# Two sets of work moved and two feeding schedules changed in a two-block transformer kernel on one core

## The chip, the cores and the metric

The kernel runs on one core of a Trainium2 chip. The core has five engines, each with its own in-order queue of instructions: TensorE (PE, matmuls and transposes), ScalarE (ACT), VectorE (DVE), GpSimd (POOL), and SyncE (SP), which here only issues DMAs. Engines wait for each other on semaphores. The metric is the device time of the core in microseconds (us), lower is better.

## The reference

Two blocks work on 256 tokens of width 1024. The first has two layers: block attention (8 heads of 128) and a pooling mixer, each followed by an MLP of width 4096. The second block is cut down here to what matters for the change:

```
u = rms_norm(h)
z, xbc, dt, q_a, c_kv, k_rope, gate_ssd, gate_mla = split(u @ w_in)
y_ssd  = ssd_branch(z, xbc, dt) @ w_ssd_out        # ends in a group-wise RMS norm of y * silu(z), 4 groups
y_mla  = latent_attention(q_a, c_kv, k_rope) @ w_mla_out   # 16 heads
merged = sigmoid(gate_ssd) * y_ssd + sigmoid(gate_mla) * y_mla
h = h + merged @ w_o
h = h + cross_attention(rms_norm(h), rms_norm(mem))        # mem: 256 x 1024
h = h + mixture_of_experts(rms_norm(h))                    # 32 experts, 2 per token
```

## The kernel before

Activations lie transposed in SBUF: channels on the 128 partitions, the 256 tokens along the free axis, so 1024 channels are 8 tiles of 128x256. Every weight matrix is streamed through a ring of four slots. To multiply float32 values exactly enough, each operand is split in two `fp32r` parts. ACT writes the high part (L1457, a copy with rounding) and DVE the low part, the remainder (L2039, source minus high part); PE then runs three matmuls for each pair of tiles (`three`, L849 to L851): high x high, high x low, low x high. A weight chunk of 1024x256 is split in two halves of 128x1024 elements. There are four buffers for such halves, so ACT can be at most four halves ahead of PE: `high_half` waits for `units_done`. In ACT's and DVE's code, `feed(n)` means: now process the next n halves. The calls of `feed` are placed by hand between the other work, and so they set the order on both engines; nothing is reordered later.

Three stages are touched.

**First attention** (`attention(MOBA, ...)`, 8 heads). DVE's loop does in step i: mask head i's scores (L2158), take the maxima (L2165), normalise head i-1 (L2177, L2179), then what `meanwhile(i)` says, which is `feed`, and at last the remainder of the output of head i-4 (L2189). ACT does in step i: the exponentials of head i (L1550), the copy of the transposed probabilities of head i-2 (L1468), `feed`, and the high part of the output of head i-3 (L1570). On PE, in step i: scores of head i, transposes for head i-2, from step 5 on one k-tile of the output projection `wo1` for head i-5, then values of head i-3.

**Latent attention's entry.** PE projects queries (`qb`, L1186) and then keys and values (`kvb`, four parts, L1209); ACT copies both out of PSUM. Value products 3 and 4 use the PSUM banks of 1 and 2, after ACT has emptied them (L1837). `ssd_roots` (L1813) computes the four square roots of the group-wise norm of the other branch. The roots and the exponentials use different function tables of ACT, so there is a table load before and one behind. DVE inverts the roots (L2476), scales z (L2482), ACT writes its high part (`z_high`, L1827), DVE its remainder (`z_low`, L2489), and PE needs that for its first `sout` product.

**mout, memT, wo2.** PE computes `mout` in four chunks, each 48 matmuls; DVE gates each and adds it to `merged` (L2599 from PSUM, L2602 an add of two tiles in SBUF); ACT writes high parts of `merged` (`norm_parts`, L1478), DVE the remainders (`low_parts`, L2052), and PE multiplies with `wo2`, k-tile by k-tile as they come. Beside it, 16 transposes (L1257) bring `mem` into the channel layout; ACT copies them out (L1468), squares them (L1521), and POOL folds the 8 tiles of squares into one with three adds (`fold`, L2882); PE sums that over partitions (L820).

Of the kernel before, what the change touches and what calls it, by code (L numbers as in the profile page):

```python
# [31 lines left out]
P = 128  # L32
# [205 lines left out]
def plan():  # L238
# [65 lines left out]
    c.fill_each("memT", 4, (2, 3, 4, 5))  # L304
    for j in range(4):
        c.load(("wo2", j), kind="cols")
    c.fill_each("wo2", 4, (4, 5), lambda j: c.done(("wo2", j)))
    c.fill(0, "norm", 8)
# [27 lines left out]
def build_two_blocks(nc, a, out):  # L336
# [3 lines left out]
    with ExitStack() as ctx:  # L340
# [172 lines left out]
        def bank(b):  # L513
            return psum[:, b, :]
# [273 lines left out]
        def _(pe):  # L788
# [460 lines left out]
            for j in range(4):  # L1249
                project_split(c.ordinal["mout", j], open_bank("mout", j), head_of=None if j else lambda k: H1 + 2 * k)  # L1250
                if j == 0:
                    pe.wait_ge(s["mem_in"], 16)
                    for i in range(4):
                        b = open_bank("memT", i)
                        for m in range(2):
                            for tb in range(TB):
                                mm = pe.transpose(bank2(b)[:, m, tb * P:(tb + 1) * P],  # L1257
                                                  mem_in[:, tb, (2 * i + m) * P:(2 * i + m + 1) * P], ident)
                        mm.then_inc(full[b], 1)
# [176 lines left out]
        def _(act):  # L1436
# [376 lines left out]
            def ssd_roots():  # L1813
                wait_made("norm", 12)
                act.activation(std[:], std[:], ACT.Sqrt, bias=eps_col[:, 2:3],
                               scale=1.0 / (4 * P)).then_inc(s["ssd_roots"], 1)
                b = wait_full("norm", 13)
                act.activation(cb_sb[:], bank(b)[:, 0:TOK], ACT.Sqrt, bias=eps_col[:, 2:3],
                               scale=1.0 / (4 * P)).then_inc(made[b], 1)
                act.activation(std_col[:, 0, 1:2], eps_col[:, 0:1], ACT.Exp)  # L1820
# [9 lines left out]
            for part in range(4):  # L1830
# [8 lines left out]
                if part == 1:  # L1839
                    ssd_roots()  # L1840
# [10 lines left out]
            feed(2)  # L1851
            for j in range(4):
                copy_out(mem[:, 2 * j:2 * j + 2, :], "memT", j)
            for j in range(4):
                if j % 2 == 0:
                    feed(1)
                squares(8, j)
            feed(2)
            norm_parts("merged")
# [155 lines left out]
        def _(dve):  # L2015
# [225 lines left out]
            for j in range(9):  # L2241
# [6 lines left out]
                if j and j % 2 == 0:  # L2248
                    rope1(j // 2 - 1)
            attention(MOBA, CAUSAL, float(P) ** -0.5, True, one_tile,  # L2250
                      lambda i: feed((2, 2, 2, 0, 1, 1)[i] if i < 6 else 0))
# [342 lines left out]
            for j in range(4):  # L2594
# [9 lines left out]
                if j == 2:  # L2604
                    low_parts("merged", 0, 6)
            low_parts("merged", 6)
# [358 lines left out]
```

## Time and profile before

| | |
|---|---|
| time of the runs | 1382.43 us median of 3 (1382.18 to 1383.81) |
| profiled execution | 1382.18 us, its span 1380.4 us |
| PE busy | 1308.7 us (95%) |
| DVE busy | 1027.6 us (74%) |
| ACT busy | 869.0 us (63%) |
| POOL busy | 77.9 us (6%) |
| mean granted TensorE clock | 0.985 |
| the 16 transposes of `mem` | 863.23 us to 864.90 us from the span's start |

Times within the execution count from the span's start. The span runs from the first to the last instruction; 1.8 us of the profiled execution lie outside it. A matmul's record is longer than its share of the time, since matmuls overlap: what counts is how far apart they start (0.12 us for 128x256 at full clock). A row of a timeline stands for consecutive alike instructions, and the idle time ahead of it is in brackets with the instruction that ended it.

### The profile page before, as it was taken

To read this page: it belongs to the slowest core of one execution; us is meant where nothing else is said; L and a number is where in the kernel's file an instruction comes from. 1 tells how busy PE (TensorE), PEld (TensorE's weight loads), DVE (VectorE), ACT (ScalarE), POOL (GpSimd) and SP (SyncE) were. 2 spreads that over 40 slices of the span, in tenths; PEclk is the share of its full clock that TensorE was granted. 3 is DMA by queue.
4 is the path that set the end of the run, shared out by engine and by line. 5 is a ranking of instruction groups with operands and counts; after the bars stand their busy time and mean duration, and the time that the engine had idled before them with its cause. 6 is when DMAs were issued, how large, how long until landed. Compare 5 with 4: busy or idle time off the path is not lost.

```text
span 1380.4 us, 23725 instructions
## 1 busy us (share of the span) xinstructions
PE 1308.7 (95%) x9379; PEld 1202.8 (87%) x9382; DVE 1027.6 (74%) x1518; ACT 869.0 (63%) x1272; POOL 77.9 (6%) x81
## 2 busy tenths in 40 slices
PE   6999999999999998999999899999978999999993
PEld 6989999998999996999999888999976777777772
DVE  6676655568555657898988887875559999999994
ACT  5565444446444444676555766554458999999993
POOL 0000100001000000000001200110000111001113
PEclk9999999999999999999999999999989999999997
DMA  8644555553655541654544634555346999999972
GB/s 263 189 154 127 191 188 188 189 185 94 206 189 183 182 145 62 208 160 153 155 125 141 230 106 158 165 164 172 143 170 245 352 361 353 355 366 365 360 267 100
DMA packets 149676, 279.78 MB, mean 203 GB/s; under 512 B 13673, under 2 KB 122062, under 8 KB 136142
## 3 DMA queue, kind: packets, MB, share of 16 engines
q1 hardware_dynamic: 141886, 270.09, 56.8%
q0 software_dynamic: 7696, 8.41, 2.0%
q8 instruction: 63, 1.03, 0.3%
q14 instruction: 31, 0.25, 0.0%
HBM read 274.26 MB, written 21.50 MB: 214 GB/s over the span
## 4 chain that ended last, share of the span: by engine, by line
PE 74%; DVE 15%; ACT 6%; issue 3%; DMA 1%; ACTq 0%; DVEq 0%; POOLq 0%; POOL 0%; SPq 0%
PE psum L849 18%; PE psum L851 17%; PE psum L850 17%; DVE weights_parts L2627 3%; PE psum L1396 3%; PE psum L1395 3%; PE psum L1394 3%; DVE weights_parts L2039 3%; PE psum L1419 2%; ACT weights_parts L1903 2%; DVE arena L2421 2%; PE psum L1421 2%; PE psum L1420 2%; ACT weights_parts L1457 1%; ACT squares L1969 1%
## 5 line engine op out<-in xcount | busy, mean ns | idle before, releaser
L2039 DVE TENSOR_TENSOR weights_parts<-ring,weights_parts 128x1024 fp32r<-128x1024 f32 (+3 forms) x312 | 363.5, 1184 | 177.0 <-ACT weights_parts L1457 176.5
L1457 ACT ACTIVATE weights_parts<-ring 128x1024 fp32r<-128x1024 f32 (+3 forms) x312 | 308.8, 1009 | 179.3 <-PE psum L851 179.0
L849 PE MATMUL psum<-xnorm_parts,weights_parts 128*128 128x256 f32 (+1 forms) x932 | 269.8, 289 | 13.2 <-DVE xnorm_parts L2061 5.7
L850 PE MATMUL psum<-xnorm_parts,weights_parts 128*128 128x256 f32 (+1 forms) x932 | 263.3, 283 | 0.0
L851 PE MATMUL psum<-xnorm_parts,weights_parts 128*128 128x256 f32 (+1 forms) x932 | 263.1, 282 | 0.0
L849 PEld LDWEIGHTS psum<-xnorm_parts,weights_parts 128*128 128x128 f32 (+1 forms) x932 | 175.8, 189 | 20.6 <-issue 12.3
L849 PE MATMUL psum<-hidden_parts,weights_parts 128*128 128x256 f32 x640 | 181.9, 284 | 2.7 <-DVE hidden_parts L2489 1.7
L849 PE MATMUL psum<-expert_cols,weights_parts 128*128 128x256 f32 x640 | 180.7, 282 | 1.7 <-DVE expert_cols L2052 1.2
L851 PE MATMUL psum<-hidden_parts,weights_parts 128*128 128x256 f32 x640 | 180.5, 282 | 0.0
L850 PE MATMUL psum<-hidden_parts,weights_parts 128*128 128x256 f32 x640 | 180.5, 282 | 0.0
L851 PE MATMUL psum<-expert_cols,weights_parts 128*128 128x256 f32 x640 | 178.6, 279 | 0.0
L850 PE MATMUL psum<-expert_cols,weights_parts 128*128 128x256 f32 x640 | 178.6, 279 | 0.0
L850 PEld LDWEIGHTS psum<-xnorm_parts,weights_parts 128*128 128x128 f32 (+1 forms) x932 | 176.0, 189 | 1.2 <-issue 1.0
L851 PEld LDWEIGHTS psum<-xnorm_parts,weights_parts 128*128 128x128 f32 (+1 forms) x932 | 176.1, 189 | 0.3
L849 PEld LDWEIGHTS psum<-hidden_parts,weights_parts 128*128 128x128 f32 x640 | 121.4, 190 | 3.5 <-issue 3.5
L849 PEld LDWEIGHTS psum<-expert_cols,weights_parts 128*128 128x128 f32 x640 | 120.1, 188 | 2.5 <-DVE expert_cols L2052 1.4
L850 PEld LDWEIGHTS psum<-hidden_parts,weights_parts 128*128 128x128 f32 x640 | 121.3, 190 | 0.0
L851 PEld LDWEIGHTS psum<-hidden_parts,weights_parts 128*128 128x128 f32 x640 | 121.3, 190 | 0.0
L851 PEld LDWEIGHTS psum<-expert_cols,weights_parts 128*128 128x128 f32 x640 | 120.2, 188 | 0.0
L850 PEld LDWEIGHTS psum<-expert_cols,weights_parts 128*128 128x128 f32 x640 | 120.0, 187 | 0.2
L2627 DVE TENSOR_TENSOR weights_parts<-expert_raw,weights_parts 128x1024 fp32r<-128x1024 f32 x94 | 110.6, 1216 | 4.5 <-ACT weights_parts L1903 4.4
L1903 ACT ACTIVATE weights_parts<-expert_raw 128x1024 fp32r<-128x1024 f32 x94 | 94.8, 1052 | 3.0 <-PE psum L1421 2.1
(410 smaller groups left out, 2514.5 us busy)
## 6 DMA issues: line engine op xcount, KB each, us to landing
expert_raw<-in_w_exp_down SPq DMA_DIRECT2D x35, 1024.0 KB, 7.6
ring<-in_mlp_w_up SPq DMA_DIRECT2D x32, 1024.0 KB, 5.5
ring<-in_mlp_w_down SPq DMA_DIRECT2D x32, 1024.0 KB, 4.8
ring<-in_w_in SPq DMA_DIRECT2D x30, 1024.0 KB, 5.4
ring<-in_w_exp_gate SPq DMA_DIRECT2D x23, 1024.0 KB, 5.3
ring<-in_w_exp_up SPq DMA_DIRECT2D x23, 1024.0 KB, 7.6
ring<-in_attn_w_qkv SPq DMA_DIRECT2D x12, 1024.0 KB, 6.3
expert_raw<-in_w_exp_gate SPq DMA_DIRECT2D x12, 1024.0 KB, 5.0
```

Source lines behind the costliest of these rows:

```text
L849: pe.matmul(out, lh, rh, start=start, stop=False, **more)
L850: pe.matmul(out, lh, rl, start=False, stop=False, **more)
L851: return pe.matmul(out, ll, rh, start=False, stop=stop, **more)
L1394: pe.matmul(bank2(n % 2), x_high, high[:, :, k, :], start=(kk == 0), stop=False)
L1395: pe.matmul(bank2(n % 2), x_low, high[:, :, k, :], start=False, stop=False)
L1396: mm = pe.matmul(bank2(n % 2), x_high, low[:, :, k, :], start=False, stop=(kk == KT - 1))
L1419: pe.matmul(y, a_high, high[:, cc], start=(k == 0), stop=False)
L1420: pe.matmul(y, a_low, high[:, cc], start=False, stop=False)
L1457: ins = act.activation(high, src, ACT.Copy)
L1903: act.activation(high, src, ACT.Copy).then_inc(s["unit_high"], 1)
L2039: ins = dve.tensor_tensor(low, src, high.bitcast(F32), ALU.subtract)
L2627: dve.tensor_tensor(low, src, high.bitcast(F32), ALU.subtract).then_inc(s["unit_low"], 1)
```

## The change

There are four edits; the arithmetic stays the same.

- The DVE schedule of weight halves in the first attention goes from (2, 2, 2, 0, 1, 1) to (2, 2, 2, 1, 1) for steps 0 to 5.
- `ssd_roots` is no longer called after the second key and value part; its five instructions stand right after the query part on ACT.
- The transposes of `mem` stand behind the third chunk of `mout` on PE instead of the first, and use banks 0 to 3 instead of 2 to 5. ACT feeds all six weight halves first, then copies `mem`, then writes the first six high parts of `merged`, then the squares, then the last two high parts.
- DVE writes all eight remainders of `merged` after the fourth sum instead of six of them after the third.

```diff
@@ plan()
     c.fill_each("mout", 4, (0, 1, 6, 7), lambda j: c.done(("mout", j)))
-    c.fill_each("memT", 4, (2, 3, 4, 5))
     for j in range(4):
         c.load(("wo2", j), kind="cols")
     c.fill_each("wo2", 4, (4, 5), lambda j: c.done(("wo2", j)))
+    c.fill_each("memT", 4, (0, 1, 2, 3))
@@ PE
                 project_split(c.ordinal["mout", j], open_bank("mout", j), head_of=None if j else lambda k: H1 + 2 * k)
-                if j == 0:
+                if j == 2:
                     pe.wait_ge(s["mem_in"], 16)
                     for i in range(4):
                         b = open_bank("memT", i)
@@ ACT
                 feed(2)
-            def ssd_roots():
-                wait_made("norm", 12)
-                act.activation(std[:], std[:], ACT.Sqrt, bias=eps_col[:, 2:3],
...
+            wait_made("norm", 12)
+            act.activation(std[:], std[:], ACT.Sqrt, bias=eps_col[:, 2:3],
...
                 feed(1 if part < 3 else 0)
-                if part == 1:
-                    ssd_roots()
                 if part == 2:
                     z_high(0)
...
             attention(LATENT, CAUSAL, one_tile, between2)
-            feed(2)
+            feed(6)
             for j in range(4):
                 copy_out(mem[:, 2 * j:2 * j + 2, :], "memT", j)
-            for j in range(4):
-                if j % 2 == 0:
-                    feed(1)
-                squares(8, j)
-            feed(2)
-            norm_parts("merged")
+            norm_parts("merged", 0, 6)
+            squares(8)
+            norm_parts("merged", 6, KT)
             feed(4)
@@ DVE
             attention(MOBA, CAUSAL, float(P) ** -0.5, True, one_tile,
-                      lambda i: feed((2, 2, 2, 0, 1, 1)[i] if i < 6 else 0))
+                      lambda i: feed((2, 2, 2, 1, 1)[i] if i < 5 else 0))
...
                                   ALU.add).then_inc(s["y_ready"], 1)
-                if j == 2:
-                    low_parts("merged", 0, 6)
-            low_parts("merged", 6)
+            low_parts("merged")
```

The order on DVE in the first attention, from the mask of head 3 on. L2158 is the mask, L2165 the maxima, L2177 and L2179 the normalisation, L2039 a weight remainder, L2189 the remainder of an output. Before:

```order
L2158 SCALAR_TENSOR_TENSOR arena<-psum,consts_sb 128x384
L2165 TENSOR_REDUCE smax<-arena 128x1 x2
L2177 RECIPROCAL srec<-ssum 128x2
L2179 TENSOR_SCALAR arena<-arena,srec 128x128
L2179 TENSOR_SCALAR arena<-arena,srec 128x256
L2158 SCALAR_TENSOR_TENSOR arena<-psum,consts_sb 128x384
L2165 TENSOR_REDUCE smax<-arena 128x1 x2
L2177 RECIPROCAL srec<-ssum 128x2
L2179 TENSOR_SCALAR arena<-arena,srec 128x128
L2179 TENSOR_SCALAR arena<-arena,srec 128x256
L2039 TENSOR_TENSOR weights_parts<-ring,weights_parts 128x1024
L2189 TENSOR_TENSOR xnorm_parts<-psum,xnorm_parts 128x256
```

The same place in the changed kernel, whose DVE lines are numbered six lower:

```order
L2152 SCALAR_TENSOR_TENSOR arena<-psum,consts_sb 128x384
L2159 TENSOR_REDUCE smax<-arena 128x1 x2
L2171 RECIPROCAL srec<-ssum 128x2
L2173 TENSOR_SCALAR arena<-arena,srec 128x128
L2173 TENSOR_SCALAR arena<-arena,srec 128x256
L2033 TENSOR_TENSOR weights_parts<-ring,weights_parts 128x1024
L2152 SCALAR_TENSOR_TENSOR arena<-psum,consts_sb 128x384
L2159 TENSOR_REDUCE smax<-arena 128x1 x2
L2171 RECIPROCAL srec<-ssum 128x2
L2173 TENSOR_SCALAR arena<-arena,srec 128x128
L2173 TENSOR_SCALAR arena<-arena,srec 128x256
L2033 TENSOR_TENSOR weights_parts<-ring,weights_parts 128x1024
```

A weight remainder now stands ahead of head 4's mask; behind the second one the remainder of head 0's output follows, as before.

The order on ACT between the query copies and the latent attention. L1457 is a weight half, L1833 and L1834 copy keys, L1468 copies values. Before:

```order
L1457 ACTIVATE weights_parts<-ring 128x512 x4
L1833 ACTIVATE arena<-psum 64x2x256
L1834 ACTIVATE arena<-psum 64x2x256
L1457 ACTIVATE weights_parts<-ring 128x1024
L1468 ACTIVATE arena<-psum 128x512 x2
L1457 ACTIVATE weights_parts<-ring 128x1024
L1815 ACT_TABLE_LOAD
L1815 ACTIVATE std<-std,eps_col 128x768
L1818 ACTIVATE cb_sb<-psum,eps_col 128x256
L1820 ACT_TABLE_LOAD
L1820 ACTIVATE std_col<-eps_col 128x1
L1833 ACTIVATE arena<-psum 64x2x256
```

And in the changed kernel (lines one lower from here on):

```order
L1457 ACTIVATE weights_parts<-ring 128x512 x4
L1814 ACT_TABLE_LOAD
L1814 ACTIVATE std<-std,eps_col 128x768
L1817 ACTIVATE cb_sb<-psum,eps_col 128x256
L1819 ACT_TABLE_LOAD
L1819 ACTIVATE std_col<-eps_col 128x1
L1832 ACTIVATE arena<-psum 64x2x256
L1833 ACTIVATE arena<-psum 64x2x256
L1457 ACTIVATE weights_parts<-ring 128x1024
L1468 ACTIVATE arena<-psum 128x512 x2
L1457 ACTIVATE weights_parts<-ring 128x1024
```

The five instructions of the roots moved ahead of one key copy, two value copies and two weight halves.

The order on ACT behind the latent attention, from the last weight half in it. L1468 copies the transposed `mem`, L1521 squares it, L1478 writes high parts of `merged`. Before:

```order
L1457 ACTIVATE weights_parts<-ring 128x1024 x2
L1468 ACTIVATE arena<-psum 128x512 x4
L1457 ACTIVATE weights_parts<-ring 128x1024
L1521 ACTIVATE squares<-arena 128x512 x2
L1457 ACTIVATE weights_parts<-ring 128x1024
L1521 ACTIVATE squares<-arena 128x512 x2
L1457 ACTIVATE weights_parts<-ring 128x1024 x2
L1478 ACTIVATE expert_cols<-arena 128x256 x8
```

And in the changed kernel:

```order
L1457 ACTIVATE weights_parts<-ring 128x1024 x6
L1468 ACTIVATE arena<-psum 128x512 x4
L1478 ACTIVATE expert_cols<-arena 128x256 x6
L1521 ACTIVATE squares<-arena 128x512 x4
L1478 ACTIVATE expert_cols<-arena 128x256 x2
```

The squares, which POOL's fold waits for, moved behind the sixth weight half and six high parts.

## Rows read from the trace of the kernel before

**Rows 1.** The page: busy us (share), instructions of TensorE.
```profile
PE 1308.7 (95%) x9379; PEld 1202.8 (87%) x9382; DVE 1027.6 (74%) x1518; ACT 869.0 (63%) x1272; POOL 77.9 (6%) x81
```

**Rows 2.** Timeline, PE: start us, us, engine, line, what [idle before <-releaser].
```profile
99.55 0.36 PE L849 MATMUL psum<-xnorm_parts,weights_parts 128*128 128x256 f32 x1 [0.71 <-DVE xnorm_parts L2189]
...
777.14 0.36 PE L849 MATMUL psum<-hidden_parts,weights_parts 128*128 128x256 f32 x1 [1.72 <-DVE hidden_parts L2489]
...
885.54 0.38 PE L849 MATMUL psum<-expert_cols,weights_parts 128*128 128x256 f32 x1 [1.24 <-DVE expert_cols L2052]
```

**Rows 3.** Timeline, DVE, first attention, heads 3 and 4.
```profile
96.04 0.55 DVE L2158 SCALAR_TENSOR_TENSOR arena<-psum,consts_sb 128x384 f32<-128x384 f32 x1
96.63 0.61 DVE L2165 TENSOR_REDUCE smax<-arena 128x1 f32<-128x128 f32 x2
...
97.84 1.23 DVE L2039 TENSOR_TENSOR weights_parts<-ring,weights_parts 128x1024 fp32r<-128x1024 f32 x1
98.98 0.42 DVE L2189 TENSOR_TENSOR xnorm_parts<-psum,xnorm_parts 128x256 fp32r<-128x256 f32 x1
```

**Rows 4.** Timeline, ACT, first attention, same stretch.
```profile
96.77 1.04 ACT L1457 ACTIVATE weights_parts<-ring 128x1024 fp32r<-128x1024 f32 x1
...
97.98 0.39 ACT L1550 ACTIVATE arena<-arena,smax 128x128 f32<-128x128 f32 x1
...
99.23 1.05 ACT L1457 ACTIVATE weights_parts<-ring 128x1024 fp32r<-128x1024 f32 x1
```

**Rows 5.** Timeline, PE, first attention, the next two rounds' first `wo1` matmul.
```profile
102.78 0.36 PE L849 MATMUL psum<-xnorm_parts,weights_parts 128*128 128x256 f32 x1 [0.64 <-DVE xnorm_parts L2189]
...
105.12 0.36 PE L849 MATMUL psum<-xnorm_parts,weights_parts 128*128 128x256 f32 x1
```

**Rows 6.** Windows: stretch, its us, busy us of each engine, PEclk, DMA.
```profile
774.00:777.00 3.00, 0.89 (x4) 0.52 (x4) 2.97 (x5) 2.82 (x5) 0.00 (x0) 1.00 1.02 408
777.00:782.00 5.00, 4.86 (x27) 4.88 (x28) 4.88 (x11) 1.41 (x6) 0.00 (x0) 0.66 0.97 380
```

**Rows 7.** Timeline, ACT, keys, values and roots before the latent attention.
```profile
764.86 0.59 ACT L1833 ACTIVATE arena<-psum 64x512 f32<-64x512 f32 x1 [0.29 <-PE psum L851]
...
767.03 1.09 ACT L1468 ACTIVATE arena<-psum 128x512 f32<-128x512 f32 x2
...
769.08 1.28 ACT L1815 ACT_TABLE_LOAD   x1
...
773.09 0.57 ACT L1833 ACTIVATE arena<-psum 64x512 f32<-64x512 f32 x1
...
775.12 0.62 ACT L1827 ACTIVATE hidden_parts<-arena 128x512 fp32r<-128x512 f32 x1
```

**Rows 8.** Timeline, PE, the third value product's first matmul.
```profile
767.79 0.38 PE L849 MATMUL psum<-weights_parts,xnorm_parts 128*128 128x256 f32 x1
```

**Rows 9.** Timeline, DVE, the first remainder of z.
```profile
776.20 0.68 DVE L2489 TENSOR_TENSOR hidden_parts<-arena,hidden_parts 128x512 fp32r<-128x512 f32 x1
```

**Rows 10.** Timeline, PE, the first matmul of `wo2`.
```profile
882.03 0.28 PE L849 MATMUL psum<-expert_cols,weights_parts 128*128 128x256 f32 x1
```

**Rows 11.** Timeline, DVE, sums and remainders of `merged`.
```profile
873.82 2.18 DVE L2602 TENSOR_TENSOR arena<-arena,rope_a 128x512 f32<-128x512 f32 x1
...
881.16 2.10 DVE L2052 SCALAR_TENSOR_TENSOR expert_cols<-arena,expert_cols 128x256 fp32r<-128x256 f32 x6
...
883.89 0.69 DVE L2602 TENSOR_TENSOR arena<-arena,rope_a 128x512 f32<-128x512 f32 x1
```

**Rows 12.** Timeline, ACT, copies and squares of `mem`, high parts of `merged`.
```profile
864.40 2.04 ACT L1468 ACTIVATE arena<-psum 128x512 f32<-128x512 f32 x4
...
871.83 1.13 ACT L1521 ACTIVATE squares<-arena 128x512 f32<-128x512 f32 x2
...
877.51 1.32 ACT L1478 ACTIVATE expert_cols<-arena 128x256 fp32r<-128x256 f32 x4
```

**Rows 13.** Timeline, POOL, the fold's first step.
```profile
873.05 2.39 POOL L2882 TENSOR_TENSOR squares<-squares 128x1024 f32<-128x1024 f32 x1 [20.45 <-ACT squares L1521]
```

More of the change, by code:

```diff
@@ L1812, in _ @@
                 feed(2)
-            def ssd_roots():
-                wait_made("norm", 12)
-                act.activation(std[:], std[:], ACT.Sqrt, bias=eps_col[:, 2:3],
[L1816 to L1820, printed above, removed]
+            wait_made("norm", 12)
+            act.activation(std[:], std[:], ACT.Sqrt, bias=eps_col[:, 2:3],
+                           scale=1.0 / (4 * P)).then_inc(s["ssd_roots"], 1)
+            b = wait_full("norm", 13)
+            act.activation(cb_sb[:], bank(b)[:, 0:TOK], ACT.Sqrt, bias=eps_col[:, 2:3],
+                           scale=1.0 / (4 * P)).then_inc(made[b], 1)
+            act.activation(std_col[:, 0, 1:2], eps_col[:, 0:1], ACT.Exp)
             def z_high(j):
```

## The prediction

> **What bounds the kernel now.** I read the page first. TensorE (PE) is busy 1308.7 of 1380.4 us [rows 1]; the work is one in-order stream of matmuls, and ScalarE (ACT) and VectorE (DVE) matter only where PE stands still for them. Then the timelines of ACT, DVE, PE and GpSimd (POOL) around the three places that the diff touches. There the reader is to see who is the last to arrive. In the first attention PE waits for DVE's remainders before the first output-projection matmuls [rows 2]. Before the second attention it waits 1.72 us for the first remainder of z [rows 2]. In the projection `wo2` it waits 1.24 us for two late parts of `merged` [rows 2]. Everything behind each place is PE work without slack (busy 95% over the whole span), so what PE loses there reaches the end; what ACT or DVE saves there doesn't, unless it was what PE waited for.
>
> **Edit 1, first attention, DVE: a weight remainder one head earlier.** In before, DVE takes head 4's mask, maxima, reciprocal and scaling from 96.04 to 97.84 and only then the weight remainder, for which ACT's high part (96.77 + 1.04 = 97.81) is just ready [rows 3, 4]. The high part doesn't come earlier after the change, since ACT's own order stays. So DVE stands from about 96.1 to 97.84 and does the remainder at the same time as before; the 1.8 us of head work come behind it, from 98.98. The maxima of head 4 end at 98.98 + 0.59 + 0.53 = 100.1 (before 97.2). ACT's exponentials of head 4 start then instead of at 97.98, and its next weight half follows 1.25 later (97.98 to 99.23): 101.4 to 102.45. DVE, now waiting for that one a head early too, does its remainder at 102.5 to 103.6 (the 1.14 of 97.84 to 98.98), then the remainder of head 0's output, 103.6 to 104.05, which stood at 98.98. PE's first `wo1` product follows 0.15 behind: 104.2 instead of 99.55, 4.65 us late. A part comes back: DVE's next round holds no weight remainder any more. In before PE took 3.23 us from 99.55 to 102.78, waits included, where an undisturbed round takes 2.34 (102.78 to 105.12) [rows 2, 5]. So 0.9 comes back and 3.8 us stay.
>
> **The clock behind it.** PE does almost nothing from 98.5 to 104.2 (one head's three transposes). What such a hole does to the granted clock is to be seen at 774 to 782: PE had 0.89 us of work in 3 us, and in the next 5 us the clock averaged 0.66 of full [rows 6], that is about 3.4 us at 1.2 instead of 2.4 GHz and some 1.7 us of work lost. For edit 1 I take 1.5 of that (bounds 0, if the low stretch falls into the hole itself, and 2.5, if it is longer). Edit 1: 3.8 + 1.5 = 5.3 us, bounds 3 and 6.3.
>
> **Edit 2, ACT: the four roots of the normalisation with their two table loads, 4.0 us (769.08 to 773.09), moved ahead of the keys and values.** In before they stood behind the value copies. Moved, they start when the query part of ACT's queue ends, at about 764.5, and run until 768.5. Then come the key copy that started at 764.86, a weight half, and the value copies of 767.03 [rows 7], all 4.01 - 0.29 = 3.7 us later (the 0.29 us of idle goes). PE's third value product uses the bank that these copies empty: 767.79 [rows 8] becomes 771.4, +3.6 us. What gives it back is that PE had time: ACT's second key copy (773.09) now waits for PE instead, which has done 24 matmuls at 0.12 us each by 774.4. From there copy, weight half and high part of z take 2.65 (the 2.03 from 773.09 to 775.12 and the part's 0.62): 777.15. The z remainder on DVE, at 776.20 before [rows 9], starts then, 1.0 us late, and PE and the attention's first maxima with it. The reciprocal for which DVE waited on the roots is done early and gains nothing, because the high part is last now. But the 3.6 us hole of PE brings the low clock onto the products behind it: up to 1.7 us later, of which about 1.1 reach the end. Edit 2: 1.0 + 1.1 = 2.1 us, bounds 0 and 3.5.
>
> **Edit 3, PE, ACT and DVE around `mout`, `memT` and `wo2`.** PE's 16 transposes move behind the third product. PE has the same work, so `wo2` could start at 882.03 as before [rows 10]; nothing on PE. The banks that they now use were emptied long before, nothing either. The order of the other two engines is what costs. First, the remainders of `merged` 0 to 5, done at 881.16 to 883.2 in before [rows 11], all come after the fourth sum. That sum can start 1.1 us earlier (about 882.1, when PE is done, instead of 883.17, one operation of 0.72 ahead of its add at 883.89), but the first remainder now ends at 883.5 + 0.35 or later, and PE needs it for its first matmul. A remainder is 0.35 us (2.10 for 6) and three matmuls are 0.36, so PE keeps that pace: it starts near 884.0 and its wait is 2.0 instead of 1.24, +0.8 us. This is the low bound.
>
> Second, the squares of `mem` slide from 869 to 873 towards the end. ACT's sixth weight half ends at about 875.7 (PE is through three products at 874.7), the four copies take 2.04, six high parts 0.33 each, four squares 0.57 each [rows 12]: 875.7 + 2.0 + 2.0 + 2.2 = 881.9. There POOL begins its fold. In before it began at 873.05 with a step of 2.39 us, and DVE's add of two tiles in SBUF at 873.82, which takes 0.69 alone, took 2.18 [rows 11, 13]: it ended 0.56 behind POOL's step, so it stood still until POOL let go. In the new order the fold meets that add again, 0.8 us into the same step: the fourth sum, now what PE waits for. It ends near 884.9 instead of 883.5, and the first remainder meets the second step and ends near 886.3. The Trainium skill ("SBUF — State Buffer", section "SBUF: two separate sides") says that a GpSimd operation and a VectorE operation with two SBUF inputs exclude each other for a whole instruction, and whoever starts first holds the port. The row agrees with a full stop, 1.49 us, rather than a shared rate. By that rule all hangs on POOL being 0.8 us ahead; were it behind the add, the add would be free and only the remainders would pay.
>
> Worked by rows: eight remainders are 2.8 us alone, and stops in DVE's stream over that fold were 1.5 for the add and, by its neighbours, about as much again for what followed. The last remainder ends at 883.5 + 2.8 + 3.0 = 889.3, PE's first half of `wo2` at 889.8. In before it was 885.54 + 0.7 = 886.25. That is +3.5 us. PE is idle from 882.03 to 886.4 in this, longer than in any of the holes above, so the low clock follows; a part lies beside DVE's slow stream, and I add 1.1. Edit 3: 4.6 us, bounds 0.8 and 5.5. The sum of squares on PE stands behind `wo2`'s first chunk, after the fold's end (887.7), so no further wait; ACT's next weight halves come about 1 us later, and two units are still ahead of PE.
>
> **Sum.** 5.3 + 2.1 + 4.6 = 12.0 us. The profiled execution took 1382.18 us for a span of 1380.4, the median of the runs is 1382.43, so 1382.2 to 1382.4 + 12.0 = 1394.3.
>
> **On the clock rule.** The Trainium skill ("TensorE: Matmul & The Clock Gate", Part 1) says that the low clock is the default and comes back after idleness. Read strictly, as a stretch with no work at all, edit 1's hole (which holds one set of transposes) would cost nothing and the sum would be 1392.8. The row at 774 to 777 shows a fall with 0.89 us of work in it, so I go by the row.
>
> **Rivals.**
> A, the clock stays high: the three holes cost only their own length, 3.8 + 1.0 + 3.5 = 8.3, 1390.6. For it: after the 1.24 us wait at 885.54 nothing fell. Against: the new holes are two to four times longer.
> B, only the queue delays count: POOL's fold starts late enough, or early enough, not to stand before the add, and edit 2 is hidden. 3.8 + 0.8 = 4.6, 1387.0. For it: edit 2 gives 2.6 of its 3.6 us back already by my count. Against: the 0.8 us by which the fold leads is worked out from six durations of one queue.
> C, the low clock lasts longer behind two of the holes, or the low bound of give-back in edit 1 holds: 6.3 + 3.5 + 5.5 = 15.3, 1397.6.
> D, not slower: the end of the fold's present collision pays. In before the fold stops DVE by 3.1 us at 873.8 to 879.8, and this is why the fourth sum starts at 883.17 rather than 882.1. If ACT delivers its weight half for DVE in the first attention ahead of the maxima (so that edit 1 fills idle time) and PE takes the parts of `merged` as they come, 1.1 us come out of the 1.24 us wait and 0.3 from ACT's idle slot: 1381.0. It decides only if edit 1 costs under 1.4 us; against it stands ACT's row at 96.77, behind which DVE must wait.
>
> **How the numbers follow.** Forecast 0.55, A 0.20, B 0.10, C 0.09, D or no difference 0.06. A measurement of this kernel can tell about 0.2% (2.8 us) from no change. B stays above that, so slower 0.93, within 0.2% 0.05, faster 0.02. The range, 1386.5 to 1397.5, takes in the forecast with its bounds, A and B, and leaves C and D outside, 0.15 in all.
>
> **What would show it.** In the first attention PE's first `wo1` matmul 4 to 5 us later than 99.55, and a low-clock stretch near 105. The two table loads at about 764.5, PE idle for over 3 us before the third value product, and the first `hidden_parts` product 1 to 2.5 us later by this edit alone. In `wo2`, one wait of 2 to 4.5 us at its first matmul in place of the 1.24 us wait at its 19th, with POOL's first step across DVE's fourth sum. I am wrong if these waits are there but DVE or PE had slack that takes them up, or if the fold doesn't meet the fourth sum.

## The result, and the profile after

| | before | after |
|---|---|---|
| median of the runs | 1383.12 us (1382.18 to 1384.13, 4 runs) | 1397.99 us (1396.04 to 1398.29, 4 runs) |
| profiled execution, its span | 1382.18, 1380.4 | 1396.05, 1394.2 |
| PE busy | 1308.7 | 1312.1 |
| mean granted TensorE clock | 0.985 | 0.980 |

The ratio is 1.0105 with the interval [1.0089, 1.0121]: 14.9 us slower. Forecast were 12.0 us and 1394.3 us, with a range up to 1397.5. The direction and the three places are right, the size is not: the time lies 0.5 us above the range. Of the 3.7 us between forecast and measurement, 2.9 are the size of the change; 0.8 is the starting point, since the forecast started from 1382.2 to 1382.4 and the median of before is 1383.12 here.

The timeline of PE in the changed kernel, at the starts of the three places and before the third value product. The first row is the wait ahead of head 3's transposes, the first of two in the first attention; the second, fourth and fifth rows answer to [rows 2], the third to [rows 8] (start us, us, line, what, [idle before <-releaser]):

```profile
101.88 0.52 PE L898 MATMUL psum<-consts_sb,arena 128*128 128x128 f32 x3 [2.48 <-DVE arena L2173]
...
105.15 0.55 PE L849 MATMUL psum<-xnorm_parts,weights_parts 128*128 128x256 f32 x1 [2.75 <-DVE xnorm_parts L2183]
...
778.55 0.43 PE L849 MATMUL psum<-weights_parts,xnorm_parts 128*128 128x256 f32 x1 [3.63 <-ACT arena L1468]
...
786.83 0.36 PE L849 MATMUL psum<-hidden_parts,weights_parts 128*128 128x256 f32 x1 [0.20 <-DVE hidden_parts L2483]
...
895.96 0.55 PE L849 MATMUL psum<-expert_cols,weights_parts 128*128 128x256 f32 x1 [4.06 <-DVE expert_cols L2046]
```

A shift of 0.9 us was there before the first place: 0.8 of it is the load of `x`, for which PE waits at the start and which took 7.9 instead of 7.1 us. No edit touches it. So the second row stands 5.60 - 0.89 = 4.7 us later than in before. A matmul now takes 0.55 instead of 0.36 us: the clock is low.

DVE in the first attention, against [rows 3]. Two weight remainders now stand behind waits for ACT, each of 1.7 us:

```profile
98.73 1.23 DVE L2033 TENSOR_TENSOR weights_parts<-ring,weights_parts 128x1024 fp32r<-128x1024 f32 x1 [1.72 <-ACT weights_parts L1457]
99.88 0.55 DVE L2152 SCALAR_TENSOR_TENSOR arena<-psum,consts_sb 128x384 f32<-128x384 f32 x1
...
103.44 1.23 DVE L2033 TENSOR_TENSOR weights_parts<-ring,weights_parts 128x1024 fp32r<-128x1024 f32 x1 [1.71 <-ACT weights_parts L1457]
104.59 0.42 DVE L2183 TENSOR_TENSOR xnorm_parts<-psum,xnorm_parts 128x256 fp32r<-128x256 f32 x1
```

ACT before the latent attention, against [rows 7]. The roots run from 771.50, and the key copy of the last row waits for PE:

```profile
771.50 1.28 ACT L1814 ACT_TABLE_LOAD   x1
...
777.81 1.08 ACT L1468 ACTIVATE arena<-psum 128x512 f32<-128x512 f32 x2
...
783.18 0.59 ACT L1832 ACTIVATE arena<-psum 64x512 f32<-64x512 f32 x1 [3.34 <-PE psum L851]
```

DVE before `wo2`, against [rows 11]:

```profile
891.94 0.69 DVE L2593 SCALAR_TENSOR_TENSOR rope_a<-arena,psum 128x512 f32<-128x512 f32 x1 [3.79 <-PE psum L851]
892.66 1.75 DVE L2596 TENSOR_TENSOR arena<-arena,rope_a 128x512 f32<-128x512 f32 x1
894.33 4.37 DVE L2046 SCALAR_TENSOR_TENSOR expert_cols<-arena,expert_cols 128x256 fp32r<-128x256 f32 x8
```

And POOL at the same time, against [rows 13]:

```profile
891.52 4.89 POOL L2874 TENSOR_TENSOR squares<-squares 128x1024 f32<-128x1024 f32 x3 [29.20 <-ACT squares L1521]
```

POOL's fold starts 1.1 us ahead of DVE's add, which takes 1.75 instead of 0.69 us, and eight remainders take 4.37. L2593, which reads PSUM, ran beside the fold at its usual 0.69.

The granted clock in windows of the changed kernel, against [rows 6] (the columns are those there):

```profile
101.00:105.00 4.00, 0.52 (x3) 0.31 (x3) 2.25 (x7) 2.58 (x7) 0.00 (x0) 0.73 0.00 0
105.00:112.00 7.00, 6.85 (x35) 6.26 (x35) 4.22 (x16) 3.13 (x12) 0.00 (x0) 0.67 0.51 150
...
779.00:782.00 3.00, 3.00 (x16) 3.00 (x16) 2.29 (x3) 0.85 (x1) 0.00 (x0) 0.50 0.96 371
...
895.00:899.00 4.00, 3.04 (x13) 2.98 (x14) 4.00 (x9) 2.06 (x3) 1.33 (x2) 0.50 0.00 0
```

0.50 is 1.2 GHz. Adding up windows of 1 us, the low clock lasts 6.8 us from 102.9 (in before it is not low there), 3.4 us from 778.7 (as much as in before, but earlier and over products that decide) and 6.8 us from 894.7 (in before none). The first and the last of these begin while PE still waits: 2.3 and 1.2 us of them lie inside the hole, where they cost nothing. Nor does the stretch of before at this place cost anything: in the changed kernel, where the products behind z run at full clock, the shift falls from 9.7 to 8.6 us and is back at 9.7 when 6 us have passed, since PE then waits 1.4 us for ACT, a wait that before doesn't have.

Following the same PE instructions through both traces, each place costs: first attention 6.0 us (shift 0.9 to 6.9), keys and values 2.8 (6.9 to 9.7), `wo2` 5.4 (9.7 to 15.1). At the router 1.4 us come back: PE waits 6.3 us there in both, but behind it the clock is low for 10.2 us in before and 6.8 in after. 0.9 + 6.0 + 2.8 + 5.4 - 1.4 = 13.7, and the spans differ by 13.8.

### The profile page after: what moved, and what is told of

Same layout as the page of the kernel before. It is cut to its first block, busy times and chain, and to the rows that moved or that the text cites. A ratio compares the mean times of both kernels' runs of the same rounds, so it can differ in the third digit from the quotient of the medians.

```text
span 1394.2 us, 23725 instructions
## 1 busy us (share of the span) xinstructions
PE 1312.1 (94%) x9379; PEld 1206.4 (87%) x9382; DVE 1027.7 (74%) x1518; ACT 869.6 (62%) x1272; POOL 77.1 (6%) x81
## 4 chain that ended last, share of the span: by engine, by line
PE 76%; DVE 14%; ACT 6%; issue 3%; DMA 1%; ACTq 0%; DVEq 0%; POOLq 0%; POOL 0%; SPq 0%
PE psum L849 18%; PE psum L851 18%; PE psum L850 18%; DVE weights_parts L2619 3%; PE psum L1394 3%; PE psum L1395 3%; PE psum L1396 3%; PE psum L1419 2%; DVE weights_parts L2033 2%; PE psum L1421 2%; PE psum L1420 2%; DVE arena L2415 2%; ACT weights_parts L1457 1%; ACT weights_parts L1897 1%; DMA ring<-in_attn_w_qkv 1%
## 5 line engine op out<-in xcount | busy, mean ns | idle before, releaser
L1457 ACT ACTIVATE weights_parts<-ring 128x1024 fp32r<-128x1024 f32 (+3 forms) x312 | 309.0, 1010 | 186.5 <-PE psum L851 186.3
```

Of the source, the lines that this page charges most:

```text
L1457: ins = act.activation(high, src, ACT.Copy)
```

## The experiments

"At its place" is the growth of the shift against before between a PE instruction ahead of the place and one behind it, from the profiled executions; the ratio is over all runs. Kernels are built on before where not said otherwise.

**1. Each edit alone.** The edits are those of the change. e1_attention_feed:

```
-  lambda i: feed((2, 2, 2, 0, 1, 1)[i] if i < 6 else 0))
+  lambda i: feed((2, 2, 2, 1, 1)[i] if i < 5 else 0))
```

> Edit 1 alone (DVE's schedule of weight halves in the first attention, (2, 2, 2, 1, 1)), nothing else. Theory (read from the changed kernel's trace): the first output-projection matmul is 4.7 us late (waits of about 2.5 and 2.8 us ahead of it), 0.9 us of queue delay comes back, and a low-clock stretch of 6.8 us behind the hole costs 2.2 us more: +6.0 us at the end, of which up to 1.4 could come back at the router's long wait. The prediction's term was 5.3 us. Rival 1 (queue delays only, clock stays high when this edit is alone): +3.8 us. Rival 2 (the edits reinforce each other: alone it costs under 3 us).

e2_roots_early moves the body of `ssd_roots` up:

```
+ wait_made("norm", 12)
+ act.activation(std[:], std[:], ACT.Sqrt, ...)
...
- if part == 1:
-     ssd_roots()
```

> Edit 2 alone (the four square roots and their two table loads ahead of keys and values on ACT). Theory: PE waits 3.6 us before its third value product, only 1.0 us of queue delay is left at the first product with z, and the low-clock stretch behind the hole costs 1.8 us more: +2.8 us. The prediction's term was 2.1 us. Rival: since before has its own low-clock stretch at that place, the clock costs nothing net and the edit costs +1.0 us.

e3_mem_late takes all else of the change:

```
- if j == 0:
+ if j == 2:
      pe.wait_ge(s["mem_in"], 16)
...
- low_parts("merged", 6)
+ low_parts("merged")
```

> Edit 3 alone (transposes of mem behind the third product of mout, ACT's new order, all eight remainders of merged behind the fourth sum). Theory: POOL's fold starts just ahead of DVE's fourth sum and stops it; PE waits about 4.1 us at the first wo2 matmul, +3.5 us of queue delay, +1.9 us from 6.8 us of low clock: +5.4 us. The prediction's term was 4.6 us. Rival: without the 9.7 us that the other edits add ahead of it nothing changes in the relative order, so the same; were the fold's place set by something else (an input's arrival), it would miss the sum and cost +0.8 to +2 us.

Measured: 1.0045 [1.0032, 1.0058], 1.0021 [1.0013, 1.0030], 1.0039 [1.0027, 1.0051], that is 6.0 (1389.04), 2.7 (1385.76) and 5.4 us (1388.47) over 1383.03. The three add up to 14.1, close to the change's 14.9, so nothing shows that they act on each other; the intervals would hide an effect of 2 us. At their places the edits cost 6.2, 2.8 and 4.7 us.

**2. Edit 3 in two halves.** e3_remainders_last has only DVE's part, all eight remainders in one call (the last two lines above; the call for six of them behind the third sum goes too). e3_mem_late_remainders_kept has everything of edit 3 but that.

> Only DVE's part of edit 3: all eight remainders of merged behind the fourth sum, while mem's transposes, squares and POOL's fold stay where they were. Theory (the prediction's low bound): the wait at the first wo2 matmul is 2.0 us in place of 1.24 us at the 19th: +0.8 us, no collision with the fold; the clock may fall behind a 2.0 us hole, then up to +2.5. Rival: the remainders' order carries most of edit 3: +3 us or more.

> Edit 3 without DVE's part: mem's transposes, ACT's order and so POOL's fold are late, but six remainders of merged stay behind the third sum. Theory: the fold still stops DVE's fourth sum or the last two remainders, but PE has 18 wo2 matmuls to do meanwhile, so its wait stays under 3 us and sits at the 19th matmul: +1.5 us (0.5 to 2.5), with no or a short low-clock stretch. With the remainders' order alone at +0.7 to +1.5 us, the two parts would then cost less apart than together (5.4). Rival: the parts add up, and this one costs 4 us or more by itself.

Measured: 1.0011 [1.0002, 1.0020] and 1.0018 [1.0008, 1.0027]; at their place 0.7 and 1.2 us, as expected. Together they cost 4.7. While six remainders are ready early, PE has 18 matmuls to do when POOL stops DVE, and its wait, at the 19th, is 1.90 us; without them it has nothing to do and waits 4.06. The hole of 1.93 us left by the first half did not lower the clock.

**3. The holes filled.** Matmuls on zeros before the waits, into a bank that the next product starts anew. after_holes_filled, on the changed kernel:

```
+ if at is MOBA and n == 3:
+     fill_hole(open_bank("wo1", 0), 11)
...
+ if i == 5:
+     fill_hole(open_bank("wo1", 0), 12)
...
+ fill_hole(FILL["gates", 7][0], 16)
...
+ fill_hole(open_bank("wo2", 0), 18)
```

> The changed kernel with 57 matmuls on zeros (128x512 bf16, about 0.22 us each at full clock, results overwritten) in PE's three new holes: 11 before the transposes of head 3 and 12 before the first wo1 matmul (waits 2.48 and 2.75 us), 16 before the third value product (3.63 us), 18 before the first wo2 matmul (4.06 us). All waits and queues stay. Theory (the clock term was undersized): the granted clock stays at 1 behind all three holes, and with the low-clock stretches go about 2.2 + 1.8 + 1.9 = 5.9 us, of which 1.4 had come back at the router, so 4.5 net: about 1393.5 against 1398.0 for the changed kernel and 10.5 above before (queue delays 3.8 + 1.0 + 3.5 = 8.3 and what the router now loses as before). Rival 1: the clock term was right (3.7 us) and the queue delays were undersized: about 1394 to 1395 with queue delays of over 10 us still to be seen at the three places. Rival 2: the fillers only delay PE: 1398 or more.

Measured: 1389.72 against 1383.88, ratio 1.0047 [1.0033, 1.0061]. The same windows as above, now full of work and at full clock; PE's first `wo2` product still comes when DVE lets it:

```profile
105.00:112.00 7.00, 7.00 (x52) 6.64 (x53) 6.22 (x22) 4.41 (x17) 0.00 (x0) 1.00 0.52 152
...
892.00:899.00 7.00, 6.79 (x54) 6.55 (x55) 6.17 (x10) 2.76 (x4) 0.47 (x1) 1.00 0.12 21
```

At the places 3.8, 1.2 and 3.3 us are left. These are the queue delays, what the order of the work costs with the clock up, forecast as 3.8, 1.0 and 3.5. The clock's part is the difference from the unfilled kernel: 2.1 (2.3 with edit 1 alone), 1.6 and 2.1, together 5.9 where the forecast had 3.7. I had expected 10.5 over before; it was 5.8, since here too the router's low stretch is 6.8 us and gives about 1.4 back, and the rest lies within the interval.

e1_holes_filled does the same with the first two fillers and edit 1 alone.

> Edit 1 alone with 23 matmuls on zeros (11 before head 3's transposes, 12 before the first wo1 product) in its two holes of 2.5 and 2.8 us. Theory: edit 1's 6.0 us are 3.8 of queue delay and 2.2 of low clock; filled, the queue delay alone is left: +3.8 us (3.5 to 4.2) where the edit alone gave +6.0, and no low-clock stretch at 102 to 110 us. Rival: the clock term is what the prediction had, 1.5: +4.5 us.

Measured: 1.0036 [1.0022, 1.0050]; 3.8 us at its place, where edit 1 unfilled costs 6.2. PE at the first `wo1` product of the two kernels, first with edit 1 alone, where the product itself runs slow:

```profile
104.71 0.55 PE L849 MATMUL psum<-xnorm_parts,weights_parts 128*128 128x256 f32 x1 [2.76 <-DVE xnorm_parts L2189]
```

With the fillers the product starts at the same time and runs at full clock:

```profile
101.80 2.75 PE L803 MATMUL psum<-zeros 128*128 128x512 bf16 x12
104.72 0.36 PE L853 MATMUL psum<-xnorm_parts,weights_parts 128*128 128x256 f32 x1 [0.17 <-DVE xnorm_parts L2197]
```

before_holes_filled puts such matmuls into before's own holes:

```
+ fill_hole(open_bank("small", 0), 25)   # before the first win product
...
+ fill_hole(4, 7)                        # before the first product with z
...
+ fill_hole(open_bank("rank", 0), 28)    # router
```

> The kernel before with 60 such matmuls in its own holes: 25 before the first win product (wait of 5.69 us), 7 before the first product with z (1.72 us), 28 before the router's rank matmuls (6.33 us). Theory: the low-clock stretches behind them (6.8, 3.4 and 10.2 us in before) go, each low microsecond giving back half a microsecond of PE work where PE is the bound: 3.4 + 1.7 + 1 to 3 us, so about 6 us below before, 1376 to 1379. Rival 1: behind the router PE waits for ACT and DVE anyway and the win stage is bound by weight remainders on DVE: 2 us or less. Rival 2: the clock falls all the same, since the fillers end before the wait does: no change.

Measured: 0.9999 [0.9990, 1.0008], no gain; my 6 us were wrong. The low stretches behind the first filler and at z are gone, and the first gives nothing: the shift is 0.5 us ahead of the `win` stage and 0.4 behind it, because there DVE sets the pace (8.73 of the 9 us from 526 to 535 busy, where PE has 7.58). At the router a low stretch of 3.4 us is left and the time doesn't move either. And a hole of 2.0 us without a releaser (instruction issue) appeared at 761.6 to 763.6, with 3.4 us of low clock behind it; over that stage the shift grows by 2.6. So the run doesn't tell by itself what the filler at z is worth.

**4. Edit 1 with ACT in step.** e1_act_half_earlier:

```
- feed((2, 2, 0, 1, 1)[i] if i < 5 else 0)     # ACT, first attention
+ feed((2, 2, 1, 1)[i] if i < 4 else 0)
```

> Edit 1 with ACT's schedule moved as well: ACT takes its weight halves in the first attention as (2, 2, 1, 1) instead of (2, 2, 0, 1, 1), so that each is written one head before DVE asks for it. Theory (edit 1 costs because DVE stands 1.7 us, twice, before a half that ACT writes in the same round): these two waits go, the first wo1 matmul comes at about 100.6 us of the span where it is 99.55 in before and 104.7 with edit 1 alone, PE's two waits of 2.5 and 2.8 us shrink to under 1.5 us together, no low-clock stretch follows: 0 to +1 us at the end against +6.0 for edit 1 alone. Rival: it is DVE's longer queue ahead of the mask that costs, not the wait for ACT: +3 us or more.

Measured: 1.0005 [0.9996, 1.0014], 0.2 us at its place. PE's first `wo1` product:

```profile
100.58 0.36 PE L849 MATMUL psum<-xnorm_parts,weights_parts 128*128 128x256 f32 x1 [0.95 <-DVE xnorm_parts L2189]
```

It comes at 100.58 as expected, no low stretch follows, and edit 1's 6 us are gone, though DVE still has the remainder ahead of head 4's mask. The wait for ACT was the cause.

**5. Edit 2 with four value banks.** e2_four_value_banks:

```
- c.fill_each("vh", 4, (2, 3))
+ c.fill_each("vh", 4, (2, 3, 4, 5))
```

> Edit 2 with the four value products in four PSUM banks (2, 3, 4, 5) instead of two, so that the third doesn't wait for ACT's copies. Theory: PE's hole of 2.7 to 3.6 us ahead of the third value product goes, and the low-clock stretch over the products behind it with it; ACT's second key copy then waits for neither PE nor the roots and the first product with z comes 0.7 us earlier than in before, where it came 2.8 us later with edit 2: -0.7 us at the end (0 to -2). Rival: the z path on ACT is late by itself (1 us by the prediction's count, 2.8 with the clock) and stays so: +1 us or more.

Measured: 0.9997 [0.9988, 1.0007]; -0.7 us at its place, where edit 2 alone costs +2.8. The roots stand as early as in the change; without the bank's wait PE has no wait over 1.6 us there, and the clock stays high.

**6. Edit 3 without the collision.** after_fold_later, on the changed kernel:

```
+ pool.wait_ge(s["xn_ready"], XN_NO["merged"] + KT)
  fold(8, sq)
```

> The changed kernel, but POOL's fold of mem's squares waits until DVE has written all eight remainders of merged; nothing else differs. Theory (the collision carries edit 3's queue delay): DVE's fourth sum takes 0.7 us in place of 1.75, the eight remainders 2.8 in place of 4.4, PE's wait at the first wo2 matmul falls from 4.06 to about 2.0 us, the clock may stay high behind it, and the wo2 stage comes 2.7 to 4.5 us earlier; the fold meets the next weight remainders instead, which may give back 0 to 2 us. About 1394 to 1396 against 1398. Rival: the wait is set by the order of sum and remainders, and stays above 3.5 us: no change.

after_fold_and_sum_later also moves PE's sum over the squares behind `wo2`'s second chunk:

```
- if j == 0:
+ if j == 1:
      folded_sum(8, sq)
```

> The changed kernel with POOL's fold behind DVE's remainders of merged, as in the last run, and besides PE's matmul over the folded squares behind wo2's second chunk instead of its first, so that it needn't wait for the late fold. Theory: the 3.3 us wait that ate the gain in that run goes, the wait of 1.9 us at the first wo2 matmul stays, and what remains is the collision's price: 2.5 to 3.5 us below the changed kernel, about 1395. The clock may or may not fall behind the 1.9 us wait (it did in the last run, it did not in the run with DVE's part alone). Rival: the late fold now stops DVE's weight remainders, and ACT's root comes too late for the norm behind wo2: no gain.

Measured: 1.0110 [1.0094, 1.0125] and 1.0106 [1.0090, 1.0121], no gain in either; at their place they cost 7.3 and 6.7 us, where the change costs 5.4. The collision does go (DVE's add 0.69, eight remainders 2.77, PE's wait 1.94 instead of 4.06), but a wait comes for it. In the first, PE waits for the late fold:

```profile
904.27 0.45 PE L820 MATMUL psum<-squares,consts_sb 128*128 128x256 f32 x1 [3.34 <-POOL squares L2874]
```

In both POOL needs 8.3 to 8.4 us for the fold that took 4.89, and the DVE weight remainders beside it take up to 2.2 instead of 1.2 us. In the second PE waits 2.9 us for a bank that DVE empties behind the late norm. POOL's row there:

```profile
896.37 8.36 POOL L2874 TENSOR_TENSOR squares<-squares 128x1024 f32<-128x1024 f32 x3 [33.81 <-DVE expert_cols L2046]
```

So the fold is taken off POOL. e3_sum_on_pe, edit 3 alone:

```
- fold(8, sq)          # POOL
...
- folded_sum(8, sq)    # PE
+ norm_sum(8)
```

> Edit 3 alone, without POOL's fold of mem's squares: PE sums the eight tiles itself behind wo2's first chunk (eight matmuls of 0.215 us instead of one, +1.5 us of PE work). Theory: no GpSimd operation meets DVE, so the fourth sum takes 0.7 and the eight remainders 2.8 us, PE's first wait in wo2 is 1.9 us in place of 4.06, and nothing later waits: +0.7 (order) + 1.5 (matmuls) = +2.2 us, +3.9 if the clock falls behind the 1.9 us wait, against +5.4 for edit 3 with the fold. Rival: edit 3's price is not the collision: +6 us or more with the added matmuls.

> The same with eight matmuls on zeros in the 1.9 us wait before wo2. Theory: the clock stays high and +2.2 us are left whatever it did in the run without them. Rival (fillers do nothing for so short a hole): the same time as without them, with the same clock.

Measured: 1.0032 [1.0020, 1.0044] and with the filler 1.0025 [1.0015, 1.0036]. DVE in edit 3 with the fold:

```profile
883.76 0.69 DVE L2596 SCALAR_TENSOR_TENSOR rope_a<-arena,psum 128x512 f32<-128x512 f32 x1 [3.79 <-PE psum L851]
884.48 1.75 DVE L2599 TENSOR_TENSOR arena<-arena,rope_a 128x512 f32<-128x512 f32 x1
886.15 1.49 DVE L2049 SCALAR_TENSOR_TENSOR expert_cols<-arena,expert_cols 128x256 fp32r<-128x256 f32 x1
```

And without it:

```profile
884.04 0.69 DVE L2599 TENSOR_TENSOR arena<-arena,rope_a 128x512 f32<-128x512 f32 x1
884.65 0.75 DVE L2049 SCALAR_TENSOR_TENSOR expert_cols<-arena,expert_cols 128x256 fp32r<-128x256 f32 x2
```

At its place this costs 3.5 us, not 2.2: I had read one sum matmul as 0.215 us, but each is two passes, and sixteen take 3.6, so the added work is 3.0 and about 0.5 is left for the order. The clock stayed high behind the 1.93 us hole, so the filler had nothing to save (3.7 at its place). Edit 3's 4.7 at its place are then 3.3 with the clock up (experiment 3), of which 0.5 to 0.7 are order and some 2.6 the collision, and 1.4 of clock (3.4 us low).

**7. All cures on the changed kernel.** after_mended joins 4, 5 and the two moves of 6.

> All three at once on the changed kernel: ACT's halves one head earlier in the first attention, four banks for the value products, fold and sum behind the remainders. Theory: the three causes are independent and complete: 0 to +1 (first attention), -0.7 (z), +0.8 with the clock up or +2.7 with it down (wo2): 0 to +3 us against before, 11 to 14 below the changed kernel. Rival: a part of the loss has another cause, or the cures bring new waits: +5 us or more against before.

Measured: 1.0035 [1.0021, 1.0048], 5.6 us over before, so the rival holds. Between the first attention and the end of the latent attention the shift goes from 0.4 to 0.0 us, as the cures promise (0.2 and -0.7); `wo2` costs 8 us, because the two moves of 6 were no cure.

**8. A version below before.** before_best has the edits of 4 and 5 and this:

```
-     low_parts("merged", 0, 6)
- low_parts("merged", 6)
+     low_parts("merged", 0, 4)
+ low_parts("merged", 4)
```

> A version from what the runs showed: edit 1 with ACT's halves one head earlier (+0.1 at its place), edit 2 with four value banks (-0.7 at its place), and of edit 3 only this: four remainders of merged behind the third sum and four behind the fourth, instead of six and two, so that the fourth sum starts 0.7 us earlier. Theory: PE's wait of 1.24 us at the 19th wo2 matmul becomes about 0.8 at the 13th and the last remainder ends 0.4 us earlier: -1.0 us in all against before, near what a measurement can tell. Rival: PE reaches the fourth remainder before DVE has the sum, and the wait grows: +0.5 us or more at wo2, no change in all.

Measured: 1381.60 (1380.47 to 1382.37, 11 runs) against 1383.72, ratio 0.9987 [0.9978, 0.9996]. PE's wait of 1.24 us in `wo2` [rows 2] has become

```profile
885.42 0.38 PE L849 MATMUL psum<-expert_cols,weights_parts 128*128 128x256 f32 x1 [0.71 <-DVE expert_cols L2049]
```

At the places it gains 0.7 (z) and 0.5 (`wo2`) and loses 0.2 (first attention), the 1.0 us expected; by the interval the whole is worth 0.6 to 3.0 us. It is the only kernel here whose interval lies below before.

## Why the prediction was right and where not

**Edit 1.** Queue delay 4.65 - 0.9 = 3.8: measured 4.7 at the first product and 3.8 at its place with the clock up. Right, and its cause (DVE stands before ACT's half) is shown by experiment 4. The clock was put at 1.5 and cost 2.1 to 2.3.

**Edit 2.** The roots at 764.5 (771.50 less the shift of 6.9: 764.6), PE's hole of 3.6 (3.63), 1.0 us of queue delay (1.2): right. That the bank's wait is the cause is shown by experiment 5. The clock was put at 1.1, with only a part of 1.7 reaching the end; it cost 1.6, about half of the 3.4 us low, since the slowed products are those that ACT's key copy waits for. So the first product with z came 2.8 us later by this edit, where the prediction's sign was 1 to 2.5.

**Edit 3.** Fold at 881.9 (891.52 less 9.7: 881.8), the stopped sum, 3.5 us (3.3 with the clock up): right. The last remainder was put at 889.3 and came at 898.7 - 9.7 = 889.0. The clock was put at 1.1 and cost 2.1.

**The step that failed** is the size of the clock terms: 1.5 + 1.1 + 1.1 = 3.7 us in the sum, measured 5.9. There are two errors in it. For edits 1 and 3 I took the single low stretch of 3.4 us as the pattern, but the low clock lasted 6.8 us at both. Of edit 1's, 4.5 us lay on work behind the hole, which at half speed is the 2.1 to 2.3 measured. Of edit 3's, 5.6 us lay on work, or 2.8 us at half speed, and 2.1 were paid: "a part lies beside DVE's slow stream" was right, but the 1.1 beside it was half of what came. For edit 2 the stretch was the 3.4 us assumed and the discount was wrong: "of which about 1.1 reach the end", where nearly all of the 1.7 did. The prediction's bounds held the longer stretch (2.5 for edit 1), the values taken did not. That length isn't fixed either: edit 3 alone, with the same wait of 4.06 us, had 3.4 us of low clock and cost 4.7 at its place instead of 5.4. What makes it one or the other stays open.

8.3 + 5.9 = 14.2, less the router's 1.4 and plus the 0.9 there before the first place, gives 13.7; the profiled spans differ by 13.8. The router's 1.4 was not foreseen. The medians differ by 1.1 us more than the profiled pair, which is within the interval and has no place in a trace.

The first half of rival C, a longer low clock behind two of the holes, is what happened. That its 1397.6 comes nearest to the 1397.99 measured is partly luck: its 15.3 us are over the 14.2 found at the places, and before's median stood 0.7 to 0.9 us above its starting point. From that starting point the measured 14.9 us would have ended at 1397.2, just inside the range, whose upper end also lay 0.1 us below the sum of the prediction's own upper bounds. So the 0.5 us beyond the range say little; the 2.2 us missing in the clock terms are the error.

**On the clock rule.** Edit 1's hole held one set of transposes, and still the clock fell, at 102.9, in the second of its two waits. The Trainium skill ("TensorE: Matmul & The Clock Gate", Part 1), read strictly, would have had it stay; the row decides. The same part says of the slow matmuls at a kernel's start that their number varies from run to run of one kernel, and that they can be left out of a model as under 1% of a typical span. Variation between runs is seen here too: the mean granted clock of before_best's 11 runs goes from 0.984 to 0.990. The share holds also for the three new holes (5.9 of 1394 us), but it misleads for a change: it was 5.9 of 14.2.

**On the lock.** DVE's add of two SBUF tiles ended 1.06 us late behind POOL's step, and the sum that reads PSUM was not touched. That agrees with the exclusive lock of the Trainium skill ("SBUF — State Buffer", section "SBUF: two separate sides"). POOL's 8.36 us in experiment 6 show the lock from its other end: there POOL waits as well.

## What to carry to other kernels

Where two engines process the same list by hand-placed calls, compare their orders item by item: a consumer moved one step ahead of its producer waits a whole step, and the engine behind both loses more. Price a new TensorE hole as what is left of its length when the waits behind it have shrunk (1.2 of 3.63 us at edit 2), plus half of that part of the low-clock stretch which falls on work that decides. The stretches behind holes of 2.7 to 5 us here were 3.4 or 6.8 us long, with up to 2.3 us inside the hole. Before moving an operation off a collision, ask whom it meets at its new place: twice here the cure cost what it saved.

## What the runs showed of the hardware

Whether a hole of 1.5 to 2 us lowers the clock is not set by its length. The same 1.47 us hole of PE (instruction issue, before L1051) stands in all 18 traces, in before at 324.3 to 325.8 us. There the clock stays up behind it (the columns are those of [rows 6]):

```profile
326.00:331.00 5.00, 5.00 (x32) 4.58 (x31) 3.71 (x10) 2.24 (x6) 0.00 (x0) 1.00 0.46 186
```

In before_best, where that hole is as long and ends at 325.75, it falls, and PE gets 22 matmuls done instead of 32:

```profile
326.00:331.00 5.00, 5.00 (x22) 4.38 (x22) 2.15 (x7) 1.28 (x4) 0.00 (x0) 0.66 0.44 181
```

It fell in 3 of the 18 and cost 1.4 to 1.7 us each time. Of the six traces with a hole of 1.90 to 1.94 us before or in `wo2` it fell in three. The router's 6.3 us hole had 6.8, 10.2 or 13.7 us of low clock behind it, worth about -1.4, -0.2 to +0.2 and +0.4 to +0.8 us. It would be easy to put the spread of 2 to 5 us among runs of one kernel down to such throws, but the runs of before give it no support: over 83 of the 84 that were taken beside the experiments, time and mean granted clock have a correlation of -0.04. (The one left out has a mean clock of 0.934 and took 1386.21 us.) In before_best's 11 runs it is -0.84. What else spreads the runs of before stays open. Low clock also costs nothing where DVE sets the pace: filling before's 5.7 us hole ahead of the `win` stage removed 6.8 us of it and gained nothing.
